# Three pairs' query roots taken at once, a decay table multiplied together, and key-value products by head, in a two-block transformer kernel

## The reference

```python
n = rms_norm(h, attn_norm_w[l])
proj = n @ w_in[l]
aq, ak, av, rq, rk, rv, rg = jnp.split(proj, split_at, axis=-1)
aq = rope(rms_norm(aq.reshape(B, S, ATTN_HEADS, HEAD_DIM), q_norm_w[l]), pos)
ak = rope(rms_norm(ak.reshape(B, S, ATTN_KV_HEADS, HEAD_DIM), k_norm_w[l]), pos)
y_attn = windowed_gqa_sink(aq, ak, av, attn_sink[l])
...
dmat = jnp.where(mask[None], jnp.exp(lg * jnp.maximum(diff, 0.0)[None]), 0.0)
inner = jnp.einsum('bhcnd,bhcmd->bhcnm', qc, kc) * dmat[None, :, None]
kv = jnp.einsum('bhcmd,bhcme->bhcde', kc * zeta[None, :, None, :, None], vc)
r = g_chunk * r + kv_c
```

## Time and profile before

| | us |
|---|---|
| median of 3 runs (lowest, highest) | 2879.9 (2877.08, 2881.48) |
| the profiled execution: its time | 2877.56 |
| its span, first to last instruction | 2875.4 |
| PE busy in the span | 2764.6 (96%) |
| DVE, ACT, POOL busy | 1598.0, 919.8, 1331.7 |
| mean granted TensorE clock | 0.987 of full speed |

### The profile page before, as it was taken

One profiled execution on the slowest core, in us unless ns is written; L12 is line 12 of the kernel. 1 busy time (PEld: TensorE's weight loads), 2 busy tenths in 40 slices (PEclk: granted clock), 3 DMA queues, 4 the chain that ended last, 5 costly groups with the idle time before them and its releaser, 6 DMA issues. The chain is left out here.

```text
span 2875.4 us, 36743 instructions
## 1 busy us (share of the span) xinstructions
PE 2764.6 (96%) x13796; PEld 2236.2 (78%) x13796; DVE 1598.0 (56%) x2470; ACT 919.8 (32%) x1771; POOL 1331.7 (46%) x1012
## 2 busy tenths in 40 slices
PE   7899999999999999999999899999899999999997
PEld 6677787778888888787766688878777788888886
DVE  6676775675555555633367731143378655555555
ACT  5744422232222222323344410021243322223222
POOL 3223243456665666633222244446513666566663
PEclk9999999999999999999999999999999999999998
DMA  3000102111111111131101011131101111111111
GB/s 131 30 30 30 42 16 88 52 45 51 60 52 48 56 52 59 37 118 30 45 23 38 30 44 52 51 120 64 66 16 44 52 63 48 52 52 52 63 48 66
DMA packets 71375, 151.94 MB, mean 53 GB/s; under 512 B 6448, under 2 KB 29360, under 8 KB 70064
## 3 DMA queue, kind: packets, MB, share of 16 engines
q1 hardware_dynamic: 64256, 123.76, 13.5%
q10 hardware_dynamic: 6960, 26.01, 2.4%
HBM read 141.36 MB, written 8.39 MB: 52 GB/s over the span
## 5 line engine op out<-in xcount | busy, mean ns | idle before, releaser
L649 POOL TENSOR_TENSOR WH<-WRAW,CST 128x512 fp32r<-128x512 f32 x204 | 228.3, 1119 | 888.9 <-PE PS L774 765.3
L772 PE MATMUL PS<-XH,WH 128*128 128x512 f32 x1248 | 513.3, 411 | 2.7 <-DVE XL L2086 2.7
L774 PE MATMUL PS<-XH,WL 128*128 128x512 f32 x1248 | 490.5, 393 | 0.0
L773 PE MATMUL PS<-XL,WH 128*128 128x512 f32 x1248 | 489.9, 393 | 0.0
L683 POOL TENSOR_TENSOR WL<-WRAW,WH 128x512 fp32r<-128x512 f32 x216 | 310.0, 1436 | 272.8 <-ACT WH L1714 271.9
L2528 DVE TENSOR_TENSOR H<-H,PS 128x512 f32<-128x512 f32 x352 | 236.1, 684 | 161.9 <-PE PS L1094 159.4
L772 PEld LDWEIGHTS PS<-XH,WH 128*128 128x128 f32 x1248 | 235.9, 189 | 82.1 <-issue 36.1
L1092 PE MATMUL PS<-HH,WH 128*128 128x512 f32 x704 | 275.7, 392 | 5.3 <-DVE HL L2462 5.3
L1714 ACT ACTIVATE WH<-WRAW 128x512 fp32r<-128x512 f32 x204 | 129.0, 632 | 472.1 <-PE PS L1094 383.6
L651 POOL TENSOR_TENSOR WL<-WRAW,WH 128x512 fp32r<-128x512 f32 x204 | 271.2, 1330 | 16.0
L774 PEld LDWEIGHTS PS<-XH,WL 128*128 128x128 f32 x1248 | 235.9, 189 | 52.1
(11 more groups left out here) (331 smaller groups left out, 5019.4 us busy)
## 6 DMA issues: line engine op xcount, KB each, us to landing
WRAW<-ws SPq DMA_DIRECT2D x104, 512.0 KB, 3.4
WRAW<-ws SPq DMA_DIRECT2D x176, 256.0 KB, 2.6
RAWX<-ws SPq DMA_DIRECT2D x88, 256.0 KB, 2.7
H<-xT ACTq DMA_DIRECT2D x4, 1024.0 KB, 11.0
H<-xT ACTq DMA_DIRECT2D x2, 2048.0 KB, 9.6
h_spill<-H ACTq DMA_DIRECT2D x1, 4096.0 KB, 11.6
H<-h_spill ACTq DMA_DIRECT2D x4, 1024.0 KB, 9.0
outT<-H ACTq DMA_DIRECT2D x4, 1024.0 KB, 4.4
```

What stands on the lines that cost most here:

```text
L649: pool.tensor_tensor(WH[:, j, c], WRAW[:, j, c], ONES[:, 0:1].to_broadcast((P, 512)), ALU.mult).then_inc(hi_split, 1)
L772: pe.matmul(out, WH[:, j, w], rh(kt), start=(n == 0), stop=False)
L773: pe.matmul(out, WH[:, j, w], rl(kt), start=False, stop=False)
L774: last = pe.matmul(out, WL[:, j, w], rh(kt), start=False, stop=(n == len(kts) - 1))
```

## The change

Three edits in one. First, `after1` on ACT takes a root only for the first q unit; for the others it copies the sums to `RTQ`, and one `Sqrt` of 48 columns follows in step 6, with one DVE reciprocal in step 7. Second, ACT makes the decay table as two exponentials per head, forward into `DT` and backward into a new tile `DB`, in two parts of four heads, and DVE multiplies them (`exp(a)*exp(b)` for `exp(a+b)`); `XI` moves from step 33 to 34, and `r_decays(1)` waits until DVE has read `DB`. Third, `r_kvs` makes eight products of 64x64 in place of four of 128x128, packed into 256 columns, and `r_fold` takes one instruction of 128 partitions.

```diff
--- before.py
+++ after.py
@@ -268,6 +268,7 @@
             DT = sb(st, "DT", [P, 2, 4, P])
             BST = sb(st, "BST", [P, NB, 4, 64])
             TST = sb(st, "TST", [P, 4, 64])
+            DB = sb(st, "DB", [P, 2, 2, P])
         with ExitStack() as st:
             sb(st, "gap0", [P, 16 * S])
             ROOM = sb(st, "ROOM", [P, 2 * S])
@@ -355,7 +356,7 @@
             "r_turned", "r_kz", "r_kv", "r_state", "r_qx", "r_in", "r_si", "r_out", "r_copied"))
         r_sq, r_sum, r_root, r_inv, r_spread, r_norm = map(sem, ("r_sq", "r_sum", "r_root", "r_inv", "r_spread", "r_norm"))
         gate_th, gated, turned_heads, rst_made = map(sem, ("gate_th", "gated", "turned_heads", "rst_made"))
-        head_inv, key_done = map(sem, ("head_inv", "key_done"))
+        head_inv, key_done, query_root, r_dec = map(sem, ("head_inv", "key_done", "query_root", "r_dec"))
 
 
         prod, w_sum, w_high, w_high0, w_low = map(sem, ("prod", "w_sum", "w_high", "w_high0", "w_low"))
@@ -945,8 +946,10 @@
                 if t >= 2:
                     pe.wait_ge(r_state, t if t >= 7 else t - 1)
                 for j in range(4):
-                    last = pe.matmul(PS[:, bank, blk(j)], KZ[:, t % 2].rearrange("p h d -> p (h d)")[:, blk(j)],
-                                     RV[:, c, blk(j)], start=True, stop=True)
+                    for hh in range(2):
+                        d = j * P + 64 * hh
+                        last = pe.matmul(PS[64 * hh:64 * hh + 64, bank, 64 * j:64 * j + 64], KZ[:, t % 2, 2 * j + hh],
+                                         RV[:, c, d:d + 64], start=True, stop=True)
                 last.then_inc(r_kv, 1)
 
             def r_inner(c):
@@ -1572,7 +1575,11 @@
                         dst, src = query_norm(u - U_Q1, 4 * h, 8), PS[:, MB, 0:8]
                     else:
                         dst, src = key_root(h), PS[:, MB]
-                    act.activation(dst, src, ACT.Sqrt, scale=1.0 / 64, bias=v(V_EPS)).then_inc(m_free, 1)
+                    if u > U_Q1:
+
+                        act.activation(dst, src, ACT.Copy).then_inc(m_free, 1)
+                    else:
+                        act.activation(dst, src, ACT.Sqrt, scale=1.0 / 64, bias=v(V_EPS)).then_inc(m_free, 1)
                 elif kind == "v":
                     act.wait_ge(m_full, nm.n + 1)
                     nm.n += 1
@@ -1602,6 +1609,13 @@
                 flat = PS[:, SB:SB + 2, :].rearrange("p a b -> p (a b)")
                 act.activation(PT1[:].rearrange("p a b -> p (a b)")[:, 0:nk * 2 * P], flat[:, 0:nk * 2 * P],
                                ACT.Copy).then_inc(pt_ready, 1)
+
+            def r_decays(m):
+                for n in range(4 * m, 4 * m + 4):
+                    j, hh = n // 2, n % 2
+                    act.activation(DT[:, hh, j], CST2[:, 0:P], ACT.Exp, scale=v(V_LFB + n))
+                    last = act.activation(DB[:, hh, j % 2], CST2[:, P:2 * P], ACT.Exp, scale=v(V_LBB + n))
+                last.then_inc(r_dec, 1)
 
             for g in range(46):
                 if g == 2:
@@ -1623,18 +1637,22 @@
                     copy_turned1(s - 1)
                 if g >= 2:
                     after1(g - 2)
+                if s == 6:
+                    act.wait_ge(m_free, 12)
+                    act.activation(RTQ[:, 16:64], RTQ[:, 16:64], ACT.Sqrt, scale=1.0 / 64, bias=v(V_EPS)).then_inc(query_root, 1)
                 if s == 32:
                     act.dma_start(CST2, cst[:, C_DIF1:NCONST]).then_inc(cst2_in, 16)
                 if s == 33:
                     act.wait_ge(cst2_in, 16)
+                    r_decays(0)
+                if s == 34:
                     for d in range(2):
                         for j in range(4):
                             c = (C_XF, C_XB)[d] - C_DIF1
                             last = act.activation(XI[:, d, j], CST2[:, c:c + P], ACT.Exp, scale=v((V_LF, V_LB)[d] + j))
                     last.then_inc(r_tab_a, 1)
-                if s == 35:
                     act.wait_ge(r_tab_d, 1)
-                    act.activation(DT[:], DT[:], ACT.Exp).then_inc(r_tab_a, 1)
+                    r_decays(1)
 
 
             def r_copy(c):
@@ -2193,6 +2211,8 @@
                 if kind == "q":
                     j = u - U_Q1
                     dve.tensor_tensor(Q1[:, j, half(h)], a, r, ALU.add).then_inc(proj_done, 1)
+                    if j:
+                        return
                     dve.wait_ge(m_free, g + 1)
                     dve.reciprocal(query_norm(j, 4 * h, 8), query_norm(j, 4 * h, 8)).then_inc(head_inv, 1)
                 elif kind == "k":
@@ -2222,8 +2242,8 @@
                 if s == 0:
                     dve.wait_ge(mask_in, 16)
                     dve.wait_ge(vec_ready, 1)
-                if b in (0, 4):
-                    dve.wait_ge(head_inv, 2 * j + b // 4 + 1)
+                if s in (0, 4, 8):
+                    dve.wait_ge(head_inv, s // 4 + 1)
                 if s >= 2:
                     dve.wait_ge(turned, s - 1)
                 p = prob(s)[:, :, 0:nk]
@@ -2254,14 +2274,12 @@
                 dve.tensor_copy(Q1[:, j, blk(b)], PS[:, OB, 0:P]).then_inc(o_out, 1)
 
 
-            def r_decay(n):
-
-                j, hh = n // 2, n % 2
-                link(dve.tensor_scalar(DT[:, hh, j], CST2[:, 0:P], v(V_LFB + n), None, ALU.mult))
-                ins = dve.scalar_tensor_tensor(out=DT[:, hh, j], in0=CST2[:, P:2 * P], scalar=v(V_LBB + n),
-                                               in1=DT[:, hh, j], op0=ALU.mult, op1=ALU.add)
-                if n == 7:
-                    ins.then_inc(r_tab_d, 1)
+            def r_decay(m):
+
+                dve.wait_ge(r_dec, m + 1)
+                dt = DT[:, :, 2 * m:2 * m + 2]
+                ins = dve.tensor_tensor(dt, dt, DB[:], ALU.mult)
+                ins.then_inc(r_tab_d, 1)
 
             def r_weigh(t):
                 dve.wait_ge(r_turned, t + 1)
@@ -2282,20 +2300,16 @@
                 if t == 0:
                     dve.wait_ge(proj_done, 26)
                 dst = BST[:, c - 1] if d else FST[:, (c + 1) % 2]
+                kv = PS[:, bank, 0:256].rearrange("p (a b) -> p a b", a=4)
                 if t in (0, 7):
-                    for r in (slice(0, 64), slice(64, 128)):
-                        last = dve.tensor_copy(dst[r], PS[r, bank].rearrange("p (a b) -> p a b", a=4)[:, :, r])
-                    last.then_inc(r_state, 1)
+                    dve.tensor_copy(dst, kv).then_inc(r_state, 1)
                     return
                 if not d and c >= 1:
                     dve.wait_ge(r_out, c)
                 dve.wait_ge(r_state, t)
                 prev = BST[:, c] if d else FST[:, c % 2]
                 link(dve.tensor_tensor(TST[:], prev, GC[:, d].unsqueeze(2).broadcast_to((P, 4, 64)), ALU.mult))
-                for r in (slice(0, 64), slice(64, 128)):
-                    last = dve.tensor_tensor(dst[r], TST[r], PS[r, bank].rearrange("p (a b) -> p a b", a=4)[:, :, r],
-                                             ALU.add)
-                last.then_inc(r_state, 1)
+                dve.tensor_tensor(dst, TST[:], kv, ALU.add).then_inc(r_state, 1)
 
             def r_inverse(h):
                 dve.wait_ge(r_root, h + 1)
@@ -2312,7 +2326,7 @@
 
             def r_inside(c):
                 if c == 0:
-                    dve.wait_ge(r_tab_a, 3)
+                    dve.wait_ge(r_tab_d, 2)
                     dve.wait_ge(full[2], uses[U_WO1 - 1][2] + 1)
                 if c >= 2:
                     dve.wait_ge(r_out, c - 1)
@@ -2330,6 +2344,9 @@
                     key_norm(0)
                 if g == 6:
                     key_norm(1)
+                if s == 7:
+                    dve.wait_ge(query_root, 1)
+                    dve.reciprocal(RTQ[:, 16:64], RTQ[:, 16:64]).then_inc(head_inv, 1)
                 if 0 <= s < 32:
                     soft1a(s)
                 if g >= 2:
@@ -2344,10 +2361,8 @@
                             r_weigh(t)
                         if 1 <= t < 8:
                             r_fold(t - 1)
-                        if t == 1:
-                            dve.wait_ge(cst2_in, 16)
-                        for n in ((), (0, 1), (2, 3), (4,), (5,), (6,), (7,), (), ())[t]:
-                            r_decay(n)
+                        if t in (2, 5):
+                            r_decay(t // 3)
                         if t == 8:
                             r_inside(0)
             for c in range(NB):
```

## The result

| | before | changed kernel |
|---|---|---|
| median of the runs shown | 2878.49 us (2876.99 to 2881.48, 4 runs) | 2858.34 us (2857.05 to 2859.46, 4 runs) |
| profiled execution, span | 2877.56, 2875.4 us | 2857.05, 2854.9 us |
| mean granted clock of that span | 0.987 | 0.987 |

What follows compares the result with a forecast made beforehand. PE, busy 96%, was taken as the bound, waiting in the attention steps on a ring through ACT and DVE. Terms -15.2 (roots), -5.0 (decay table) and +1.2 (products) sum to -19.0 us, giving 2860.0 us, range 2853 to 2870.

Steps and rivals of the forecast that it cites:

- roots, steps 1 to 6: Attention steps 1 to 6: 67.28 us would fall to 51.71 without waits, the excess of 15.57 us going.
- roots, step 7: Attention step 7: the `Exp` load stands in the ring, 8.3 us against 7.8 of PE work; charged 0.4 us.
- decay table, with the low clock behind its wait: Last projection slots: waits of 2.63 and 0.7 us and 1.68 us of low clock go, -5.0 us.
- products by head: Seven groups in projection slots and seven in the loop: 16 records near the upper bound of 1.02 us, +1.2 us.
- a ring longer than PE's slot: Attention steps: evacuation, loads, root, DVE's reciprocal and normalising outlast PE's slot; without roots 7.5 us against 8.82 of PE work.
- both waits for `KZ`: Last projection slots: PE's waits for DVE's `KZ`, 3.2 us in all, 2.5 of it at `t` = 3; predicted to go.
- DVE's wait for the exponentials: Projection, `t` = 2 and 5: possible new wait in `r_dec` for ACT's exponentials; slack given as 2 us.
- streaming matters little and I take near the upper bound: +1.2: Products by head: two-column head sums take 0.10 us a record, 128 columns 0.12; bounds -5.5 to +1.7 us.
- the one with cheap products: Rival on products by head: lower bound holds, 6.7 us better than the term, 2853; chance 0.12.
- The dear rival: Products by head: array shape changes make groups dear, +47 us, 2906, slower, chance 0.03; mild form 2866, chance 0.06.
- the low stretches of the earlier trace: Clock near half, 0.56 and 0.50, after PE's longest waits, in step 6 and behind `t` = 3; predicted to go.
- The ring too long: Rival on attention steps: stretched instructions make the ring 8.5 of 8.8 us, some waits stay, 2866; chance 0.14.

Runs made afterwards that it cites:

- two kernels that kept one half of the ring each: First edit with DVE's wait and a scratch reciprocal kept: 2868.37 us; first edit with ACT's table loads kept by a one-column root: 2868.23 us.
- the table alone: Only the second edit, the decay table as a product, on the kernel before: 2874.73 us, ratio 0.9986.
- the run with 128 columns: Changed kernel with products by head streaming all 128 columns and the old fold of two instructions: 2864.97 us, 6.4 above the changed kernel.
- the first edit alone: Only the first edit, the roots of three pairs together, on the kernel before: 2868.83 us, ratio 0.9964.
- the products by head alone: Only the third edit, products by head and one fold instruction, on the kernel before: 2873.71 us, ratio 0.9985.
- the kernel with the loads kept: First edit plus a one-column scratch root before each of ACT's six copies, so table loads stay without DVE's wait: 2868.23 us, ratio 0.9958.

## Why the prediction was right, and which terms were not

The time and its sign were right, and two of the three mechanisms. That the total came within 1.1 us is in part luck: the term of the products was off by 3.8 us, even in its sign, and the clock, which was in no term, gave 2.8 back:

| term | forecast | by the trace |
|---|---|---|
| roots, steps 1 to 6 | -15.6 | -15.0 |
| roots, step 7 | +0.4 | 0.0 |
| decay table, with the low clock behind its wait | -5.0 | -5.3 |
| products by head | +1.2 | -2.6 |
| low clock in other places | not in the sum | +2.8 |
| sum | -19.0 | -20.1 |

The span's own difference is -20.5; the 0.4 between lie in the loop, where the landmarks give 2.4 us for the products' 2.0.

**The roots.** Right, and by the mechanism named: a ring longer than PE's slot. I computed 51.71 us for steps 1 to 6 without waits, and they take 52.25; the 0.5 missing are in steps 2 to 5, 8.94 us where I had 8.82. Evacuation to copied transposes takes 93.86 + 0.79 - 89.09 = 5.56 us in step 2, where I had 5.69. The rest of the ring, which I had estimated at 1.8 us, takes 98.04 - 96.19 = 1.85 us from PE's values to the next evacuation. The ring is thus 7.4 us, and the copied transposes lie ready 1.5 us (94.65 to 96.19) before PE comes to its values:

```profile
96.19 0.88 PE L893 MATMUL PS<-PT,V 128*64 128x128 f32 x12
```

The two kernels that kept one half of the ring each show that it needed the other.

One thing the prediction left out. The steps before took 11.09, 12.09, 10.63, 11.96, 9.62 and 11.89 us, and the ring as I read it doesn't tell why every second one is longer. DVE's normalisation at the start of steps 2, 4 and 6 took 1.67, 1.66 and 2.33 us instead of 0.75 while POOL was splitting weights, and the small instruction ahead of it 0.5 instead of 0.1. They stand between the reciprocal and the next evacuation, so they lengthened the ring: up to 4.7 of the 15 us (an estimate: what these instructions took longer, 3.4 and 1.3 us). In the changed kernel DVE has such long instructions too (1.14 us at 91.37 for 0.16), but they fall into the slack. That POOL is the cause is not shown; no run moves its work. The kernel before, at step 2 and, for comparison, at step 3:

```profile
90.63 1.30 POOL L651 TENSOR_TENSOR WL<-WRAW,WH 128x512 fp32r<-128x512 f32 x1
```

```profile
90.80 1.67 DVE L2248 TENSOR_SCALAR XX<-XX,STAT 128x384 f32<-128x384 f32 x2
...
102.35 0.75 DVE L2248 TENSOR_SCALAR XX<-XX,STAT 128x384 f32<-128x384 f32 x2
```

**Step 7.** I charged 0.4 us for the load in the ring. The copied transposes come at 138.62, PE gets to its values at 138.79, and the step's length is what it was (7.78 for 7.81): nothing, by a margin of 0.17 us. The load takes 1.28 us and the exponential starts 0.01 us behind it (135.44 + 1.28 = 136.72, next start 136.73). The drain of 1.38 us, which the Trainium skill ("ScalarE: Activation LUTs", "What ACT_TABLE_LOAD costs") adds to a load, does not show here; the trace decides, as it did in the prediction.

```profile
138.79 0.88 PE L893 MATMUL PS<-PT,V 128*64 128x128 f32 x12
```

**The decay table.** Right. What is left of PE's waits is the bank's; the table alone takes both waits for `KZ` away. From the first slot's transposes (352.71 us before, 339.28 now) to those of `t` = 8 the changed kernel gains 19.3 - 13.4 = 5.9 us, and seven groups of products have 0.6 of it, so 5.3 are this term. DVE's wait for the exponentials never comes: ACT's second eight end at 353.85 us and DVE multiplies at 356.47, a slack of 2.6 us where I had given 2.

**The products by head.** The step that failed is "streaming matters little and I take near the upper bound: +1.2". I took it from the head sums, which stream two columns and take 0.10 us a record; but those have weights of 128 columns, and these have 64. And the 0.12 that I compared it with is from the loop: in a slot four products with 128 streamed columns take 0.81 us, just what the head sums take. So with 128-column weights streaming did matter little, and I carried that over to 64-column weights, for which the run with 128 columns shows that it does not hold. A group of 16 records takes 0.62 us, 0.039 a record, and the run with 128 columns 1.02. The group costs 0.19 less in a slot and 0.37 less in the loop, and 0.1 comes back in the transposes before it, so that it makes 7 x 0.09 + 7 x 0.28 = 2.6 us. Of my rivals, the one with cheap products was nearer than the forecast on this point. The change of the array's shape, of which the Trainium skill ("TensorEngine Tiling (Array Packing)", "Key Properties") says that it drains TensorE, may be those 0.1 us, which is how much longer the transposes ahead of the group take now; behind the group it is 0.02 us at most (2.17 us to the next transposes, 2.15 before). No run separates the drain from other causes. The dear rival, from 1.4 us a group, is far away.

**The clock.** I let the low stretches of the earlier trace rows vanish and put the chance of others in the range only. Those two do vanish, and others come: 1.6 us in 60 to 65 us, in code that no edit touches, and 1.2 between the loop's end (21.7 us gained) and the end of the span (20.5). In the first edit alone they came back with 5 us. That the one behind `KZ` went because the wait went is likely but not shown (see the products by head alone).

**What the other rivals said.** The ring too long (2866) fell: no step of 2 to 5 is over 9 us, and PE waits for ACT nowhere in it.

## What to carry to other kernels

Where a step of a pipeline is longer than its work, follow the ring through all engines once, from an evacuation to the next, and compare its length with the slot of the busiest engine. Here it took both, two table loads on ACT and a wait on DVE, to make every step longer, and doing the roots once for three pairs removed both. Price small matmuls by a row with the same columns of weights as well as the same streamed columns: a record with the one and not the other was off by 1.6 and by 2.6 times here (0.064 and 0.10 us for 0.039). And when a saving is below 1%, measure it at the places where it should be as well as in the total, for the clock's low stretches move with everything.

## What the runs showed of the hardware that was not expected

- A float32 record with 64-column weights runs every 0.039 us with 64 streamed columns and every 0.064 with 128 (0.62 and 1.02 us for 16). With 128-column weights it is 0.10 us with two streamed columns and also with 128 in a slot (0.81 us for 8), and 0.12 with 128 in the loop.
- DVE's normalisation of 2 x 384 columns takes 0.75 us, but 1.67, 1.66 and 2.33 us at 90.80, 113.39 and 134.96 us of the trace before, and 2.42 at 87.39 in the kernel with the loads kept, each time while POOL ran its lines 649 and 651.
- Stretches at a lower granted clock, of which 0.50 to 0.56 is read in windows of 2 us inside them (the 1.2 GHz level), move from kernel to kernel. Before, they came behind PE's waits of 2.1 and 2.5 us; but behind the same wait of 2.1 us in the kernel with the products by head alone there is none, and none behind 1.65, and one lies in 60 to 65 us of the changed kernel with 1.00 there in the kernel before. The one behind `t` = 3 cost 1.7 us, that in step 6 only 0.25. What decides where these fall stays open.
